# A mixer layer with 32 experts on one core: a weight ring of twelve pieces, a float32 gather of the token rows, and another order in the last two experts

## The reference

```python
x = x + mixed @ w_out                              # x1, 256 x 1024
h = rmsnorm(x, norm2_g)
logits = h @ w_router + b_router                   # 256 x 32
top_v, top_e = top_k(logits, 4); gates = softmax(top_v)
for e in range(32):                                # tokens that chose e
    gu = h[tok] @ w_gate_up[e] + b_gate_up[e]      # 1024 x 2048 weights
    gate, up = min(gu[:, :1024], 7), clip(gu[:, 1024:], -7, 7)
    act = gate * sigmoid(1.702 * gate) * (up + 1)
    out[tok] += gate_of_token * (act @ w_down[e] + b_down[e])   # 1024 x 1024
x = x + out
```

## Time and profile before

| | |
|---|---|
| runs | 1095.05, 1094.94, 1093.09 us; median 1094.94 us |
| the profiled execution's own time | 1094.92 us |
| its span | 1093.2 us |
| mean granted TensorE clock | 0.993 |
| PE busy | 1030.3 us, 94% of the span |
| DVE, ACT, POOL busy | 189.7, 125.7, 11.2 us |
| moved by DMA | 424.57 MB, mean 388 GB/s |

### The profile page before, as it was taken

How to read it: one execution, slowest core, us unless ns; L and a number is a source line. 1 busy time by engine, 2 the same in 40 slices (tenths; PEclk the granted TensorE clock), 3 DMA queues, 4 the chain that set the end, 5 groups by cost and what they waited for, 6 DMA issues and landing times.

```text
span 1093.2 us, 14242 instructions
## 1 busy us (share of the span) xinstructions
PE 1030.3 (94%) x5955; PEld 408.5 (37%) x5955; DVE 189.7 (17%) x470; ACT 125.7 (11%) x264; POOL 11.2 (1%) x23
## 2 busy tenths in 40 slices
PE   9999999999999999999999999999999999999997
PEld 5755564333333333333323333333333333233332
DVE  2143333011111111111001111111111110111111
ACT  2034431000100000000000000000000000000000
POOL 1000010000000000000000000000000000000000
PEclk9999999899999999999999999999999999999999
DMA  9942655899999999999999999999999999999995
GB/s 347 356 188 78 245 222 232 365 428 427 428 427 430 427 428 428 427 428 429 428 427 428 428 428 428 428 427 429 427 429 428 428 428 428 427 429 426 427 427 239
DMA packets 40191, 424.57 MB, mean 388 GB/s; under 512 B 6304, under 2 KB 7368, under 8 KB 15464
## 3 DMA queue, kind: packets, MB, share of 16 engines
q1 hardware_dynamic: 40152, 424.23, 92.6%
q10 hardware_dynamic: 16, 0.00, 0.0%
HBM read 423.18 MB, written 1.05 MB: 388 GB/s over the span
## 4 chain that ended last, share of the span: by engine, by line
PE 59%; DMA 39%; DVE 1%; issue 0%; ACT 0%; DVEq 0%; SPq 0%
DMA ring<-in_w_gate_up 35%; PE bank L1425 20%; PE bank L1456 14%; PE bank L1113 5%; PE bank L1397 4%; DMA ring<-in_w_down 4%; PE bank L1371 3%; PE bank L1299 3%; PE bank L1413 2%; PE bank L1443 1%; PE bank L1135 1%; PE bank L1147 1%; PE bank L1434 1%; PE bank L1185 1%; PE bank L1386 0%
## 5 line engine op out<-in xcount | busy, mean ns | idle before, releaser
L1425 PE MATMUL bank<-ring,ht 128*64 128x512 f32 x2048 | 455.9, 596 | 49.5 <-DMA ring<-in_w_gate_up 49.3
L1425 PEld LDWEIGHTS bank<-ring,ht 128*64 128x64 f32 x2048 | 139.1, 137 | 364.1 <-issue 263.9
L1456 PE MATMUL bank<-ring,ht 128*64 128x512 f32 x1024 | 229.3, 600 | 2.5 <-DMA ring<-in_w_down 2.5
L1050 DVE TENSOR_SCALAR mix_t<-bank 128x512 f32<-128x512 f32 x32 | 22.1, 692 | 763.9 <-PE bank L1425 763.9
L1456 PEld LDWEIGHTS bank<-ring,ht 128*64 128x64 f32 x1024 | 71.3, 138 | 157.3 <-issue 133.3
L1397 PE MATMUL bank<-ht,hn 64*128 64x512 f32 x256 | 71.7, 639 | 0.7 <-ACT ht L741 0.7
L725 ACT ACTIVATE hn<-bank 128x256 f32<-128x256 f32 x32 | 12.3, 384 | 516.1 <-PE bank L1434 516.1
L1113 PE MATMUL bank<-ring,ht 128*128 128x512 f32 x128 | 58.9, 600 | 0.0
L1371 PE MATMUL bank<-pick,parts 128*128 128x64 bf16 x1536 | 50.0, 193 | 0.0
L1371 PEld LDWEIGHTS bank<-pick,parts 128*128 128x128 bf16 x1536 | 49.1, 98 | 0.3
L741 ACT ACTIVATE ht<-bank 128x512 f32<-128x512 f32 x32 | 19.1, 597 | 245.6 <-PE bank L1456 245.6
(11 more groups left out here) (194 smaller groups left out, 395.0 us busy)
## 6 DMA issues: line engine op xcount, KB each, us to landing
ring<-in_w_gate_up SPq DMA_DIRECT2D x128, 2048.0 KB, 37.2
ring<-in_w_down SPq DMA_DIRECT2D x64, 2048.0 KB, 40.2
ring<-in_w_in SPq DMA_DIRECT2D x5, 2048.0 KB, 15.7
ring<-in_w_out SPq DMA_DIRECT2D x1, 4096.0 KB, 13.4
ring<-in_w_in SPq DMA_DIRECT2D x2, 1024.0 KB, 8.5
ring<-in_attn_bias SPq DMA_DIRECT2D x1, 1536.0 KB, 18.8
xres<-in_x SPq DMA_DIRECT2D x2, 512.0 KB, 3.8
out<-xres SPq DMA_DIRECT2D x4, 256.0 KB, 2.2
```

What stands on the lines that cost most here:

```text
L1050: dve.tensor_scalar(gate_c, bank[0][:, :], LIMIT, None, ALU.min).then_inc(gate_cut, 1)
L1425: mm = pe.matmul(bank[h][c * CAP:(c + 1) * CAP, :], xe_t[:, k, :], w[:, k % RUN, at:at + BANK], start=False, stop=(k == KD - 1), skip_grou ...
L1456: mm = pe.matmul(bank[6][c * CAP:(c + 1) * CAP, :], turned[:, at:at + CAP], w[:, k % DRUN, c * BANK:(c + 1) * BANK], start=(k == 0), stop= ...
```

## The change

Four things are changed together.

1. The ring has twelve slots, of 2 MB each (`PIECES` 9 to 12); the loops over experts have two experts a lap in place of three. The buffers that stood beside the ring are moved into slots 9 and 11 as long as the mixer runs, or overlaid on small buffers. SP issues twelve pieces by hand ahead of its loop.
2. The gather reads the float32 rows of `xres` (x1) itself; the factor of the norm is put into `pick`, which is float32 now. A gather is 8 x 2 = 16 float32 matmuls. `parts` and all that made it are gone.
3. The routing is done for the two halves of the tokens one after the other, the place of a token (`pos`) comes from PE without a mask step, and `take(0)` and `gather(0)` stand ahead of the gates.
4. At the end, down(31) goes to a PSUM bank of its own (bank 0), its first half ahead of the spread of expert 30, and the last piece is loaded in two halves.

```diff
-PIECES = 9
+PIECES = 12
-LAP = 3
-LAPS = 9
+LAP = 2
+LAPS = 14
-TINT = (0, 1, 2)
+TINT = (1, 0)
-WARM = (12, 2, 12, 2)
+WARM = (12, 2, 4, 2)
...
@@ sync: loads ahead of the loop
             sp.wait_ge(m_num, HM)
             load_gu(1, 0, 6)
             load_gu(1, 1, 7)
+            sp.wait_ge(half_mixed, 1)
+            load_gu(1, 2, 8)
+            sp.wait_ge(m_num, HM)
+            load_gu(1, 3, 9)
             sp.wait_ge(mix_m, HM)
             sp.dma_start(bdn, b_down[0]).then_inc(ld_bdn, 16)
             sp.wait_ge(mixed, 4)
-            load_gu(1, 2, 8)
+            load_d(1, 0, 10)
+            sp.wait_ge(logits, T)
+            load_d(1, 1, 11)
...
@@ gpsimd, scalar and vector: the making of parts is gone (POOL 4 operations, ACT 4, DVE 4)
-                pool.tensor_tensor(hn[:, t, 0:n], hn[:, t, 0:n], parts[:, t, 0, 0:n], ALU.subtract).then_inc(rest_1, 1)
...
@@ vector
+            dve.tensor_copy(pos[:, :, :], bank[ACC[2]][:, 0:T * NE].rearrange("p (t n) -> p t n", t=T)).then_inc(pos_ready, 1)
+            dve.wait_ge(pos_ready, 1)
+            def take(e):
+                for t in range(T):
+                    ins = dve.tensor_scalar(pick[:, t, :], slot[:, 0:CAP], pos[:, t, bass.ds(e, 1)], rs2[:, t:t + 1],
+                                            ALU.is_equal, ALU.mult)
+                ins.then_inc(picked, 1)
+            take(0)
...
@@ tensor
             def gather(n):
                 pe.wait_ge(picked, n + 1)
                 for k in range(KD):
                     for t in range(T):
-                        for i in range(3):
-                            q, j = k // RUN, k % RUN
-                            rows = parts[:, t, i, q * RUN * P:(q + 1) * RUN * P].rearrange("p (m j) -> p j m", j=RUN)[:, j, :]
-                            mm = pe.matmul(bank[7][:, k * CAP:(k + 1) * CAP], rows, pick[:, t, :],
-                                           start=(t + i == 0), stop=(t == T - 1 and i == 2))
+                        q, j = k // RUN, k % RUN
+                        rows = xres[:, t, q * RUN * P:(q + 1) * RUN * P].rearrange("p (m j) -> p j m", j=RUN)[:, j, :]
+                        mm = pe.matmul(bank[7][:, k * CAP:(k + 1) * CAP], rows, pick[:, t, :],
+                                       start=(t == 0), stop=(t == T - 1))
                 mm.then_inc(gathered, 1)
...
                 if meanwhile:
                     meanwhile(0)
+                    meanwhile(1)
                 else:
                     spread(now - 1, tint(n - 1 if n else NE - 1), 0)
                 turn_act(now, bank[6])
...
                 gate_up(base, 0, n + 1, round_no)
-                down(now, 0, n, round_no, act_t)
                 turn_slots(now + 1, bank[7])
+                down(now, 0, n, round_no, act_t, ks=range(DRUN))
                 turn_act(now + 1, bank[7])
+                down(now, 0, n, round_no, act_t, ks=range(DRUN, KD))
+                down(now + 1, 0, n + 1, round_no, last_t, bank[0], range(DRUN))
                 for t in range(T):
                     spread(now, tint(n), t)
-                down(now + 1, 0, n + 1, round_no, last_t)
+                down(now + 1, 0, n + 1, round_no, last_t, bank[0], range(DRUN, KD))
...
+            gather(0)
+            pe.wait_ge(gates_ready, 1)
+            for t in range(T):
+                mm = pe.transpose(bank[6][0:NE, t * P:(t + 1) * P], gate[:, t, :], ident[:, :])
```

More of the change, by code:

```diff
@@ L100 @@
 PIECE_LOADS = [len(range(s, KINDS * NE, PIECES)) for s in range(PIECES)]
-TINT_LOADS = [sum(tint(n) == u for n in range(NE)) for u in range(3)]
+TINT_LOADS = [sum(tint(n) == u for n in range(NE)) for u in range(len(TINT))]
 def tints_before(n):
@@ L117, in sem @@
             return ctx.enter_context(nc.semaphore(name))
-        ring = sb("ring", [P, (PIECES + 1) * PIECE])
+        ring = sb("ring", [P, PIECES * PIECE])
         def gu_half(s):
@@ L131, in layer_kernel @@
         win = ring[:, 0:4 * PIECE].rearrange("p (b k n) -> p b k n", b=WINS, k=KD)
-        wout = ring[:, 8 * PIECE:10 * PIECE].rearrange("p (k n) -> p k n", k=KD)
+        wout = [ring[:, s * PIECE:(s + 1) * PIECE].rearrange("p (k n) -> p k n", k=4) for s in (8, 10)]
         half = 4 * PIECE
@@ L138, in in_second_half @@
             place[0] += words
-            assert place[0] <= 2 * half
+            assert place[0] <= 8 * PIECE
             return ring[:, at:at + words]
@@ new lines, in layer_kernel @@
+        gate_t = s_sb[0:NE, 1, :]
+        brow = sb("brow", [P, len(TINT), BANK])
+        pickg = sb("pickg", [P, T, 2 * CAP])
+        pick = sb("pick", [P, T, CAP])
+        gate_buf = sb("gate_c", [P, BANK])
+        gate_c = gate_buf[:, :]
+        wif = gate_buf[:, 0:KD * 2 * HM].rearrange("p (k n) -> p k n", k=KD)
+        vec_r = gate_buf[0:ROWS, KD * 2 * HM:KD * 2 * HM + P]
+        if_c = gate_buf[:, P + KD * 2 * HM:P + (KD + T) * 2 * HM].rearrange("p (t s h) -> p t s h", t=T, s=2)
+        eq, eqg = (gate_buf[:, i * T * TOPK * NE:(i + 1) * T * TOPK * NE].rearrange("p (t j e) -> p t j e", t=T, j=TOPK)
+                   for i in range(2))
@@ L457, in free_of, with next_gu @@
                 return gu_used, GUN * base + GUN * m + was + 1
-            def next_gu(base, far, n, first=0):
-                if not first:
-                    sp.wait_ge(brow_used, base + far + n - 1)
-                    load_brow(far + n, tint(n))
-                for h in range(first, GUN):
+            def next_gu(base, far, n):
+                sp.wait_ge(brow_used, base + far + n - 1)
+                load_brow(far + n, tint(n))
+                for h in range(GUN):
                     used, count = free_of(base, n, h)
@@ L1415, in gate_up @@
                 mm.then_inc(brow_used, 1)
+            def gate_up(base, lap, n, round_no):
+                now = base + LAP * lap + n
+                tinted(base, lap, n, round_no)
                 pe.wait_ge(xe_ready, now + 1)
@@ L1444, in turn_act, with down @@
                 mm.then_inc(act_turned, 1)
-            def down(now, lap, n, round_no, turned):
+            def down(now, lap, n, round_no, turned, dst=bank[6], ks=range(KD)):
                 pe.wait_ge(act_t_ready, now + 1)
-                for k in range(KD):
+                for k in ks:
                     s = piece_of(n, GUN + k // DRUN)
@@ L1472, in expert @@
                 turn_act(now, bank[6])
-                if meanwhile:
-                    meanwhile(1)
-                else:
+                if not meanwhile:
                     spread(now - 1, tint(n - 1 if n else NE - 1), 1)
```

287 lines of the change are left out of this document (121 added, 166 removed).

## The result

The changed kernel takes **1107.61 us** (median of 4 runs, 1103.77 to 1108.78), the kernel before 1094.99 (1093.09 to 1095.91, 4 runs): ratio **1.0111** with the interval 1.0083 to 1.0140, so it is slower by 1.1%. Forecast were 1103.6 us and a range of 1093 to 1115. The profiled execution took 1108.35 us for a span of 1106.5.

A forecast was written before the change was run, and what follows sets the result against it. PE was taken to bind from expert 0 to the end: 211.5 us to expert 1, 830.9 for 29 experts at 28.65, 59.5 from gate_up(30) on, 1.7 around the span, giving 1103.6 us; range 1093 to 1115.

The forecast's parts named there:

- The gather's price: Gather in each expert: 32 float32 passes at 0.112 us cost 3.6 us, 2.2 us more than before.
- The stationary load sets it: Gather on PE: a float32 pass costs about 0.11 us from 8 to 129 moving columns, whatever the column count.
- the same stride of two does not show in the bfloat16 gather: Gather's strided stationary: reason for taking 0.112 us a pass, with nothing added for the stride of two.
- the bounds given: Gather: price of one float32 pass between 0.108 and 0.147 us, the upper from the stride-four transpose of activations.
- PE binds from expert 0 to the end: Expert loop: PE needs 28.65 us an expert against the DMA's 29.40, and with twelve pieces in stock never catches the loads.
- The start: Up to expert 1: half clock through the gather, gate_up(0) from 173.5 to 189.6, expert 1's gate_up at 211.5 us.
- some 3.5 us less: Last two experts: reordering leaves at worst half of down(31) after the last landing; counts only if the loads bind.
- rival A: Gather: stationary loads hide, a pass falls under about 0.08 us, the loads bind again; 1077 to 1085 us, chance 0.11.
- B's clock falls: Expert loop: thin work halves the clock in three to six experts, 3.4 us each; 1114 to 1124 us; rival B's chance 0.13.
- C's kept clock: Start: the clock does not fall before expert 0; end 1096 us with one fall in expert 0, 1092 with none; chance 0.08.
- 14.7 us for the early loads: Ring of twelve: three more pieces issued while the DMA stands still, 3 x 4.90 us sooner by the loads alone.

The follow-up runs named there:

- half_columns: The changed kernel with each gather matmul cut in two of 32 moving columns, 64 passes in place of 32: 1362.78 us in one run.
- moving_x: The changed kernel with the gather turned round: pick stationary, 512 columns of x1 moving, 8 float32 passes, then four transposes: 1079.27 us, ratio 0.9839 to the kernel before.
- f32_ring9: The kernel before, nine slots, with only the gather made float32 (pick holds the norm's factor): 1111.35 us, ratio 1.0134.
- bf16_ring12: The changed kernel with 48 bfloat16 gather passes on x1's upper halves in place of 32 float32 ones, values not the layer's: 1076.98 us, ratio 0.9839.
- contiguous: The changed kernel with the gather's stationary columns side by side, no stride, features in wrong order: 1101.95 us, ratio 1.0046 to the kernel before.
- after_again: The changed kernel itself, unaltered, run once more as reference for the clock experiments: median 1109.01 us, ratio 1.0102 to the kernel before.
- warm_gap: The changed kernel with four keep-warm matmuls just ahead of the first gather: median 1102.32 us, ratio 1.0045 to the kernel before.
- moving_x_old_end: moving_x with the last two experts in the order of before, last piece still loaded in two halves: 1080.39 us, ratio 0.9847 to the kernel before.
- late_three: moving_x with three early-issued pieces waiting for expert 0's use again, the one ahead of them for the residual: 1089.27 us, ratio 0.9934 to the kernel before.

## Why the prediction held, and where it was off

**The gather's price decided it, as predicted.** "The stationary load sets it": half_columns shows that 32 columns cost what 64 do, and moving_x that the cost goes when the wide operand moves. f32_ring9 shows that this term alone makes the loss, and bf16_ring12 that without it the kernel gains 1.6%. The size was 0.112 a pass and 28.65 an expert; measured are 3.71/32 = 0.116 and 28.80. The step that was mis-sized is "the same stride of two does not show in the bfloat16 gather": contiguous shows that with float32 it costs 0.006 a pass. It lay inside the bounds given (0.108 to 0.147). Times 29 experts it is 29 x 0.15 = 4.3 us, nearly all of what the profiled execution took above the forecast: 1106.5 against 1101.9 of span.

**PE binds from expert 0 to the end: right.** No DMA in the chain of the loop, PE 200.00 of 200. The last weights landed near 1073 or 1074 (1071 predicted), and the last half piece was used some 22 us after it came (17 or more predicted). From gate_up(30) to the end it took 59.9 us (59.5 predicted).

**The start: right, with two errors inside.** Gate_up(0) at 173.54 by the timeline (173.5), its end at 189.66 (189.6), expert 1 at 211.42 (211.5). The clock fell later than thought, at 164.4 and not from 159.5 on as before, so the gather began at 164.16, not 165.9. The gather's 6.90 us were as predicted, and what lies between gather and gate_up took 1.8 us longer than the working had it (2.5 to the row of gate_up, against 0.7). These two errors cancelled, which is luck. So is the moment at which the clock fell: in after_again's trace the same program falls at 159.7, where the prediction had it, and starts expert 1 at 213.27.

**The end: part 1's "some 3.5 us less" was wrong.** The order is worth nothing, whether the loads bind or not. The prediction set it at nothing for its own sum, so the time was not touched, but rival A's 1077 to 1085 held it. The term counted only the half of down(31) that no longer stands behind the last landing. It left out that the old order does its transposes and the spread while that piece lands, and that the new one, which has less to do there, waits for the piece instead (1.25 us, and 0.5 more ahead of the last spread).

**The rivals.** A's price (under 0.08 a pass) did not occur; in no gather here did float32 passes with a stationary of 128 columns cost less than 0.110 us each. "TensorE: Matmul & The Clock Gate" of the Trainium skill has about 81 ns for a matmul at N = 128 in "Back-to-back issue gap". The traces disagree for float32, with 0.112 us at 129 columns and, at 64 columns, 0.110 without stride and 0.116 with it. B's clock falls occurred only when the loads of the gather were doubled, and C's kept clock in no profiled execution with the thin float32 gather; the faster runs of warm_gap may be near it. With a cheaper gather it came: moving_x_old_end's first fall was at 189.0 and bf16_ring12's at 186.5, though moving_x, the same up to there, fell at 160.2. What A would have given was right apart from the mechanism: once the gather is cheap and the loads bind, the kernels stand at 1077 to 1080. That sum is partly luck: it had 14.7 us for the early loads, which are worth 8 to 10, and 3.5 for the end, which are worth nothing, but it left out what late_three gains over the kernel before.

## What to carry to other kernels

A float32 matmul that moves few columns costs its weight loads, not its columns: put the thin operand into the stationary place and let the wide one move, even if the result must then be transposed (here 3.71 us became 1.87 + 0.74). Before a deeper buffer is built, compare the period of the compute engine with that of the loads: a ring gains only while the loads are the slower of the two, and here 2.1 us more an expert on PE turned 1.6% of gain into 1.1% of loss. For a reordered end, write down what each order has to do while the last piece lands, the old order too.

## What the runs showed of the hardware

- A float32 stationary of 128 columns costs 0.110 us a pass side by side and 0.116 at a stride of two elements, at 64 moving columns (0.112 and 0.118 from start to start, the latter at 32 columns too); for bfloat16 48 passes take 1.40 us at a stride of two elements and 1.60 at four.
- The clock fell in the middle of the loop without a gap on PE: in half_columns PE was busy 3.00 of 3 us from 610 to 613 at 1.00, and 0.50 of 0.5 us from 617 at 0.50. Before it fell it ran passes of 32 columns; with 64 columns in half as many passes it stayed at 1.00.
- Runs of one kernel differ by up to 1%, and span times mean granted clock hardly does: 1106.5 x 0.989, 1102.0 x 0.993, 1105.1 x 0.991 give 1094.3, 1094.3 and 1095.2. In two traces of one program the clock fell at 164.4 and at 159.7, with expert 1 at 211.42 and 213.27.
